# Hi and lo part of a 16-column projection in one product per block instead of two, in a decoder layer on one core

## What is computed

```python
h = rmsnorm(x, g_pre_mix[l]) * (1.0 + sc1) + sh1
...
    proj = h @ w_in
    offs = np.cumsum(IN_SIZES)[:-1].tolist()
    gq, gk, gv, gr, ga_low, mq, mk, mv, gate_a, gate_b = jnp.split(proj, offs, axis=-1)
    log_a = jax.nn.log_sigmoid((ga_low @ w_alpha_up + b_alpha).astype(jnp.float32)) / GLA_GATE_TEMP
```

## Time and profile before

| what | us |
|---|---|
| median of 3 runs | 1485.96 |
| lowest, highest | 1483.83, 1487.79 |
| the profiled execution | 1484.98 |
| its span, first to last instruction | 1483.0 |
| PE busy in the span | 1442.9 |
| PEld busy | 1230.4 |
| DVE busy | 1102.9 |
| ACT busy | 701.1 |

### The profile page before, as it was taken

How to read it: one execution, slowest core, us unless ns; L and a number is a source line. 1 busy time by engine, 2 the same in 40 slices (tenths; PEclk the granted TensorE clock), 3 DMA queues, 4 the chain that set the end, 5 groups by cost and what they waited for, 6 DMA issues and landing times.

```text
span 1483.0 us, 19918 instructions
## 1 busy us (share of the span) xinstructions
PE 1442.9 (97%) x7430; PEld 1230.4 (83%) x7430; DVE 1102.9 (74%) x1129; ACT 701.1 (47%) x710; POOL 86.8 (6%) x177
## 2 busy tenths in 40 slices
PE   4999999999999999999999999999999999999998
PEld 2878888888888888878788888888888888888886
DVE  6989979898898988855587777777777666555445
ACT  4443444453535455424565545544544555334443
POOL 3000001010101000000000000000000000000000
PEclk9999999999999999999999999999999999999999
DMA  9999979897979877866467767677775555555553
GB/s 362 387 354 364 316 235 322 279 309 254 312 258 312 266 246 251 311 231 227 155 218 250 235 221 242 199 236 235 235 237 174 195 189 189 191 197 197 188 193 129
DMA packets 235815, 367.05 MB, mean 248 GB/s; under 512 B 11487, under 2 KB 161505, under 8 KB 234994
## 3 DMA queue, kind: packets, MB, share of 16 engines
q1 hardware_dynamic: 215824, 294.69, 59.4%
q0 software_dynamic: 18848, 69.23, 13.5%
q10 hardware_dynamic: 1090, 2.40, 0.4%
HBM read 364.18 MB, written 2.10 MB: 247 GB/s over the span
## 4 chain that ended last, share of the span: by engine, by line
PE 90%; DMA 4%; DVE 3%; ACT 1%; issue 1%; SPq 0%; DVEq 0%; ACTq 0%
PE ps L1244 89%; DMA raw<-in_w_in 2%; DVE acc L769 2%; DMA raw<-in_w_moba_out 1%; DMA adar<-in_w_ada 1%; ACT hi L453 1%; DMA ada<-in_w_ada 0%; SPq L312 0%; ACT junk L626 0%; DVE acc_b L788 0%; PE ps L1470 0%; PE ps L1401 0%; SPq L281 0%; DVE lo L759 0%; ACT yt L672 0%
## 5 line engine op out<-in xcount | busy, mean ns | idle before, releaser
L1244 PE MATMUL ps<-hT,hi 128*128 128x512 f32 x1936 | 465.8, 393 | 1.1 <-DVE hT L1114 1.1
L1244 PEld LDWEIGHTS ps<-hT,hi 128*128 128x128 f32 x1936 | 356.4, 188 | 72.0 <-issue 2.3
L453 ACT ACTIVATE hi<-raw 128x2048 fp32r<-128x2048 f32 x116 | 222.2, 1916 | 288.9 <-DMA raw<-in_w_in 193.5
L759 DVE TENSOR_TENSOR lo<-raw,hi 128x2048 fp32r<-128x2048 f32 x117 | 267.0, 2285 | 67.8 <-ACT hi L453 67.8
L1244 PEld LDWEIGHTS ps<-hT,lo 128*128 128x128 f32 x1936 | 248.2, 191 | 9.4
L1244 PE MATMUL ps<-hT,lo 128*128 128x256 f32 x1936 | 251.1, 283 | 0.0
L1199 DVE TENSOR_TENSOR lo<-raw,hi 128x2048 fp32r<-128x2048 f32 x88 | 199.1, 2290 | 29.9 <-ACT hi L717 29.1
L1244 PE MATMUL ps<-hi,hT 128*128 128x512 f32 x768 | 186.6, 396 | 0.8 <-DVE hT L832 0.8
L1244 PE MATMUL ps<-hi,asp 128*128 128x512 f32 x704 | 175.9, 389 | 0.0
L1244 PEld LDWEIGHTS ps<-hi,hT 128*128 128x128 f32 x768 | 144.1, 190 | 31.8 <-issue 1.6
L717 ACT ACTIVATE hi<-raw 128x2048 fp32r<-128x2048 f32 x88 | 165.7, 1905 | 8.4 <-DMA raw<-in_w_up 7.5
(11 more groups left out here) (203 smaller groups left out, 1265.0 us busy)
## 6 DMA issues: line engine op xcount, KB each, us to landing
raw<-in_w_up SPq DMA_DIRECT2D x176, 512.0 KB, 4.4
raw<-in_w_in SPq DMA_DIRECT2D x162, 512.0 KB, 5.6
ada<-in_w_ada POOLq DMA_DIRECT2D x128, 512.0 KB, 4.8
raw<-in_w_down SPq DMA_DIRECT2D x88, 512.0 KB, 4.2
adar<-in_w_ada SPq DMA_DIRECT2D x64, 512.0 KB, 10.3
raw<-in_w_o SPq DMA_DIRECT2D x32, 512.0 KB, 4.8
raw<-in_w_gla_out SPq DMA_DIRECT2D x16, 512.0 KB, 5.0
raw<-in_w_moba_out SPq DMA_DIRECT2D x16, 512.0 KB, 5.4
```

The costliest lines, as they stand in the source:

```text
L453: act.activation(hi[:, w % 4, :], raw[:, w % 4, :], ACT.Copy).then_inc(hi_done, 1)
L759: dve.tensor_tensor(lo[:, w % 4, :], raw[:, w % 4, :], hi[:, w % 4, :].bitcast(F32), ALU.subtract).then_inc(lo_done, 1)
L1244: return pe.matmul(out_, lhsT, rhs, start=start, stop=stop)
```

## The change

Of the 128 columns of each k block in slot 24 only 16 are wanted. VectorE now writes the remainder of these 16 into columns 32 to 47 (`LOW_AT`) of the same block of `hi`, in place of what stood there, and makes no `lo` tile for this slot. One product per block gives both: partitions 0 to 15 of bank 7 hold hi x h_hi and hi x h_lo, partitions 32 to 47 hold lo x h_hi (left half; the right half, lo x h_lo, is not read). The slot's first product waits for `lo_done` too. ScalarE makes a second evacuation (`galow_lo`), VectorE a second addition.

```diff
-    W_LOW = 24
+    W_LOW, LOW_AT = 24, 32
...
+        galow_lo = at("galow_lo", 146, [TOK])
...
                     act.activation(galow_x[0:RANK, :], ps[0:RANK, 7, TOK:], ACT.Copy).then_inc(low_x, 1)
+                    act.activation(galow_lo[0:RANK, :], ps[LOW_AT:LOW_AT + RANK, 7, 0:TOK], ACT.Copy).then_inc(low_x, 1)
...
             def split_lo(w):
                 dve.wait_ge(hi_done, w + 1)
+                if w == W_LOW:
+                    low_hi, low_raw = (t[:, w % 4, :].rearrange("p (k n) -> p k n", n=P) for t in (hi, raw))
+                    dve.tensor_tensor(low_hi[:, :, LOW_AT:LOW_AT + RANK], low_raw[:, :, 0:RANK],
+                                      low_hi[:, :, 0:RANK].bitcast(F32), ALU.subtract).then_inc(lo_done, 1)
+                    return
...
-                    dve.wait_ge(low_x, 1)
-                    dve.tensor_tensor(galow[0:RANK, :], ps[0:RANK, 7, 0:TOK], galow_x[0:RANK, :], ALU.add).then_inc(low_ready, 1)
+                    dve.wait_ge(low_x, 2)
+                    link(dve.tensor_tensor(galow[0:RANK, :], ps[0:RANK, 7, 0:TOK], galow_x[0:RANK, :], ALU.add))
+                    dve.tensor_tensor(galow[0:RANK, :], galow[0:RANK, :], galow_lo[0:RANK, :], ALU.add).then_inc(low_ready, 1)
...
                     pe.wait_ge(hi_done, w + 1)
+                    pe.wait_ge(lo_done, w + 1)
                     for k in range(KT):
                         if k >= 12 and k % 2 == 0:
                             pe.wait_ge(h_ready, k // 2 + 1)
-                        mm(ps[:, 7, :], hi[:, w % 4, P * k:P * (k + 1)], hT[:, k, :], k == 0, False)
-                    pe.wait_ge(lo_done, w + 1)
-                    for k in range(KT):
-                        ins = mm(ps[:, 7, TOK:], lo[:, w % 4, P * k:P * (k + 1)], hT[:, k, 0:TOK], False, k == KT - 1)
+                        ins = mm(ps[:, 7, :], hi[:, w % 4, P * k:P * (k + 1)], hT[:, k, :], k == 0, k == KT - 1)
```

## The result

| | before | changed |
|---|---|---|
| median, us (11 executions each) | 1485.70 | 1490.16 |
| lowest to highest, us | 1482.27 to 1487.79 | 1485.8 to 1495.0 |
| span of the profiled execution, us | 1483.0 | 1486.6 |
| mean granted clock (before: 35 executions of the first session below; changed: these 11) | 0.9951 | 0.9931 |

The changed kernel takes 1.0028 times as long, with a 95% interval of 1.0016 to 1.0040: slower by 0.28%, about 4.2 us. (The medians lie 4.5 us apart; the ratio with its interval is what the text goes by.) The forecast was 1484.0, and the range ended at 1487.3. The profiled execution of the changed kernel took 1488.34 us.

A forecast was written before the change was run, and what follows sets the result against it. TensorE's products were taken to bound the kernel: 1.92 us less in slot 24, all other terms 0, gives 1484.04 from the median 1485.96, said as 1484.0 us; range 1481.4 to 1487.3.

The forecast's parts named there:

- Term 1: TensorE, slot 24: 16 products of 128x256 fewer, at 120 ns each, free 1.92 us.
- Term 2: Slot 24's first product now waits for the remainder too; 0.42 us subtraction, ready 5.5 us early, cost 0.
- Term 3: VectorE gets about 1.8 us back at 175.9 from the smaller remainder; gain 0 on the path.
- Term 4: Longer way to galow, one more evacuation and addition; margin 5.6 us before the walpha product, cost 0.
- Term 5: DMA queues: loads come 1.92 us sooner and slow nothing near due; POOL's transfers follow VectorE's sums, which come with the products.
- rival B: Merge stage: two steps meet long ada transfers, TensorE loses 3.9 us against 1.92 gained; 1487.9 us, chance 0.06.
- Rival A: Gain absorbed by another pacer, loads at 80 to 175 us or merge's ada transfers; 1485.96 us, chance 0.14.
- C: Merge stage: ada transfers land sooner and TensorE's 1.94 us wait goes; 1482.1 us, chance 0.05.
- D: Slot 24: the removed products would be replaced by others; counted as part of the forecast, no chance of its own.

The follow-up runs named there:

- e15: The changed kernel again, unaltered, a single execution taken for a second profile; 1489.09 us.
- e1: Kernel before with the 16 lo products of slot 24 left out, nothing else changed; 1491.16 us, 1.0030 of before.
- e16: The changed kernel again, unaltered, a single execution taken for a third profile; 1490.38 us.
- e2: Changed kernel with 16 overwritten products of 128x256 put ahead of slot 24's own; 1486.37 us, 1.0001 of before.
- e5: Changed kernel with POOL's copy of the first up block held back until VectorE's four residual steps are done; 1487.71 us, 1.0019 of before.
- e12: Kernel before with only POOL's copy of the first up block held back; 1485.72 us, 1.0002 of before.
- e9: Changed kernel with 16 overwritten products of 128x256 put right ahead of the first product with Mb; 1486.71 us, 1.0005 of before.
- e13: Changed kernel with one w_ada sum of slot 29 and one of slot 31 made earlier, in slots 24 and 26; 1485.68 us, 0.9993 of before.
- e4: Kernel before with two w_ada sums moved from slots 28 and 29 to the end of the last head; 1486.05 us, 1.0011 of before.
- e3: Changed kernel with two w_ada sums moved from slots 28 and 29 to the end of the last head; 1488.44 us, 1.0019 of before.
- e6: Changed kernel with four w_ada sums, two from slots 28 and 29 and two from the merge, moved into the last head; 1489.88 us, 1.0040.

## Why the prediction was wrong

**Term 1, right in the slot, wrong in what it is worth.** The slot is 5.54 - 3.63 = 1.91 us shorter; forecast 1.92. In e15, which reached slot 24 at 181.49, 0.11 us later than before, the product with `walpha` starts at 196.09 and not at 197.92: 1.83 us sooner. The 120 ns per product hold. What failed is the step from there: "whatever slot 24 gives back is handed on by these waits to everything behind it". The estimate of 1.75 us by "TensorE: Matmul & The Clock Gate" of the Trainium skill (Back-to-back issue gap) lies 0.16 us below the 1.91 of the trace; the page itself gives that rule for a product by itself, without the time of its weight load.

**Term 2, right.** The subtraction of 256 elements took 0.42 us, as the line through 512 and 2048 elements gives, and TensorE waited for no remainder.

**Term 3, right in itself:** VectorE's saved 1.8 us gained nothing.

**Term 4, right.** Second evacuation 0.38 (forecast 0.35), additions 0.41 and 0.41, a margin of 194.46 - 188.78 = 5.7 us (forecast 5.6).

**Term 5 is the step that failed.** It said: "The transfers on POOL's queue wait for the sums of VectorE, which come with the products." They do not in this stretch. A sum needs its transfer (5.14 to 6.29 us in the chain), a transfer needs the buffer that an earlier sum leaves, and there are two buffers. This ring does not shift with TensorE. With TensorE sooner by 1.9 us VectorE waited 6.3 instead of 3.4 us for transfers, 2.9 more (6.2 in e1, 6.3 and 6.8 in e15 and e16), and Mb came no sooner. (The 6.0 us of e2, at the old pace, show that the ring can fall behind without it.) That Mb came 0.8 to 1.4 us later, measured from slot 24, is more than an absorbed gain; it is in all five profiles of this pace (changed, e1, e5, e15, e16). The one long transfer, 5.8 to 6.6 us where the kernel before had 4.0, is large enough for it. Term 5 had also said that the loads which come sooner slow nothing that is near its due time, from engines 64% busy at 181 to 187 us; in the stretch where VectorE waits the share is 0.88 (200 to 230 us) and 0.94 (230 to 260 us) in the kernel before. And rival B's argument, "both shift together by the same 1.92 us, so their phase should stay", fails in the same place: in the changed kernel the loads at 237.08 were issued 3.06 us sooner than before and the ada transfer at 237.18 only 2.77, and the order of the two turned over. I had looked for a second pacer by its waits on TensorE. A wait shows only who is late; Mb was ready 0.1 us ahead of use, and so in no list.

**Rival A, the gain absorbed (0.14), was right in kind and wrong in place:** I named the loads up to 175 us and the merge. It is the same stream of ada transfers, but at head 0. By it alone the time is that of before, 1485.96.

**Rival B** named the merge. The wait at the row sums is 4.10 us in the first profile and 1.94 before: 2.2 more, where B wanted 3.9 more. But it was 1.46 in e15, 1.82 in e16, 2.6 in e1, and 4.06 in e12, which is no slower than before. So it scatters by itself in either kernel, and the median doesn't hang on it as far as these runs show. Rivals C and D did not come. The measured 1490.16 lies above every rival's time; none of them had a cost of the clock in it.

**What makes it slower.** The record points at three things, with unequal proof.

- The wait at Mb, for nothing gained. Shown: e1 makes the loss with the pace alone (1.0030); e2 and e9 fill the time and end it (1.0001; 1.0005, its interval touches that of 1.0028); e13 makes Mb early and ends it (0.9993). By itself it costs 0.8 to 1.4 us (first column).
- The clock behind the wait. Shown in three profiles (1.6 us in e15). Over many executions it is supported, not shown: the mean granted clock is lower by 0.9951 - 0.9931 = 0.0020, an estimate of 0.0020 x 1486 = 3.0 us of the 4.2 (2.4 to 3.7 with the before of the other sessions, 0.9947 to 0.9956), and within the changed kernel's 11 executions time and clock go against each other (correlation -0.74, in e1 -0.69). They do so in kernels without the loss too (-0.88 in e4, -0.76 in e9), so the correlation doesn't tell which waits matter.
- The y stage: row sums to up took 105.4 us in the first profile and 104.0 in e16, 102.6 before. With the copy held back the change loses about 1.3 us less (e5), within the scatter. The long steps were also there in e2 and e13, which were not slower than before (in e13 with the wait of 3.1 us and the lower clock behind it), and in e15, where the clock didn't fall and the stretch was 102.6 long.

Why the copy met the steps in the profiles of the changed pace and not in before or e9 stays open. So does how the 4.2 us divide between the wait and the clock at Mb and those at the y stage; and the whole gain at the end, as against at Mb, is shown by no run with one edit (e13 is 1.0 us below before, with 1 inside its interval).

## What to carry to other kernels

Ahead of a saving on the engine that bounds, read the margins, not only the waits: for each operand that another engine makes behind the edit, when was it ready and when was it used. Where one was ready 0.1 us ahead of use and its engine is paced by transfers through two buffers, the saving ends there, and the idle time that it opens can cost clock as well (1.6 us in e15). Look also at the order in which two streams of transfers are issued: a saving that shifts only one of them can turn it over. Then move that engine's work earlier first (one table of numbers here), and the saving arrives at that place; whether it reaches the end hangs on the next place with a small margin.

## What the runs showed of the hardware

Waits of 2.1 to 3.1 us of TensorE were followed by the 1.2 GHz level in some executions and not in others of the same kernel: 2.2 us with the clock at 1.00 behind it (changed, first profile), 2.12 with 0.72 (e15), both at Mb; 3.09 for diag with 0.59 (changed) and 3.09 with the 32 products in 3.84 us (e15). Sixteen products more, written to be overwritten, cost nothing against before (e2, 1.0001), and e9, with them, came out below the changed kernel without them (1.0005 against 1.0028, the intervals overlapping by 0.0003). The page "TensorE: Matmul & The Clock Gate" of the Trainium skill (HAM oscillation) says that idle time between bursts of products brings back the lower clock. The trace agrees in three of five profiles at Mb; what decides between two executions no run here shows.

One step of VectorE with two operands in SBUF took 2.4 us instead of about 0.75 when POOL's copy of 128x2048 started beside it: the four took 4.37 to 4.39 us in the eight profiles where the copy began 1.26 to 1.94 us after the first (changed, e1, e2, e3, e6, e13, e15, e16), and 2.74 in the three where it began 2.00 to 2.15 us behind it (before, e9, e4) or after all four (e5 among others). The Trainium skill, "GPSIMD Engine Reference", says in its table of specifications that GpSimd shares its SBUF interface with VectorE and contends with instructions that have two inputs in SBUF. The trace agrees; the size of it, 1.63 us for one meeting, is from the rows.

Two streams of 512 KB transfers beside each other: a transfer of w_ada that was issued 0.2 to 0.3 us ahead of a slot's two loads took 4.0 us to land (before, e12), and 5.8 to 6.6 us when it was issued 0.1 us behind the first of them (changed, e1, e2, e5, e9, e15, e16). These are readings of nine profiles; no run moved this order alone.
